# The gate operation between the two halves of a weight remainder, in the expert loop of a two-layer decoder kernel

## What is computed

```python
def swiglu(h, w1, w3, w2):
    a = jax.nn.silu(jnp.einsum('bsd,df->bsf', h, w1)) * jnp.einsum('bsd,df->bsf', h, w3)
    return jnp.einsum('bsf,fd->bsd', a, w2)

for e in range(N_EXPERTS):
    y = y + gates[..., e:e + 1] * swiglu(h, w1[e], w3[e], w2[e])
```

## Time and profile before

| | before |
|---|---|
| median of 3 runs | 1457.12 us (1455.85 to 1460.83) |
| profiled execution, own time | 1462.09 us |
| span of its profile | 1460.3 us |
| TensorE busy | 1441.4 us (99%) |
| VectorE busy | 1133.1 us (78%) |
| ScalarE busy | 944.8 us (65%) |
| DMA | 437.21 MB, mean 299 GB/s; 377 GB/s from 600 to 1400 us |
| chain that ended last | TensorE 83%, issue 8%, DMA 4%, VectorE 4%, ScalarE 1% |

### The profile page before, as it was taken

The page is one execution under the profiler, slowest core; times in us unless marked ns, Lnnn a source line. Parts: engine busy times, 40 slices in busy tenths (PEclk is TensorE's granted clock), DMA queues, the critical chain, the costliest instruction groups (busy, mean ns, idle before and its releaser), DMA issues.

```text
span 1460.3 us, 19714 instructions
## 1 busy us (share of the span) xinstructions
PE 1441.4 (99%) x7542; PEld 1200.4 (82%) x7542; DVE 1133.1 (78%) x968; ACT 944.8 (65%) x844; POOL 35.4 (2%) x22
## 2 busy tenths in 40 slices
PE   9999999999999999999999999999999999999998
PEld 7998888888886787887888888888888888888886
DVE  6985664454476788988888898888888888898895
ACT  7633643443476766766777777777777777677774
POOL 0000000000000000000000001000000000000000
PEclk9999999999999999999999999999999999999999
DMA  9510666544542499999999999999999999999993
GB/s 360 206 58 28 237 220 219 191 172 146 176 162 83 152 362 364 386 364 348 377 368 386 391 373 380 372 375 376 386 383 372 387 393 367 386 389 372 369 391 149
DMA packets 183873, 437.21 MB, mean 299 GB/s; under 512 B 4880, under 2 KB 6416, under 8 KB 183824
## 3 DMA queue, kind: packets, MB, share of 16 engines
q1 hardware_dynamic: 180496, 426.11, 79.1%
q0 software_dynamic: 2336, 8.39, 2.1%
q10 hardware_dynamic: 992, 2.05, 0.4%
HBM read 431.29 MB, written 5.24 MB: 299 GB/s over the span
## 4 chain that ended last, share of the span: by engine, by line
PE 83%; issue 8%; DMA 4%; DVE 4%; ACT 1%; POOL 0%; DVEq 0%; ACTq 0%; SPq 0%; POOLq 0%
PE ps L272 26%; PE ps L274 25%; PE ps L273 25%; DMA raw<-in_od_moe_w 3%; DVE wlo L261 1%; PE ps L452 1%; DMA out<-arena,slot_tok 1%; ACT whi L255 1%; PE ps L991 1%; PE ps L840 0%; PE ps L1188 0%; DVE hTlo L316 0%; PE ps L2102 0%; DVE small L1418 0%; PE ps L333 0%
## 5 line engine op out<-in xcount | busy, mean ns | idle before, releaser
L261 DVE TENSOR_TENSOR wlo<-raw,whi 128x2048 fp32r<-128x2048 f32 x406 | 905.8, 2272 | 170.6 <-ACT whi L255 168.3
L255 ACT CAST whi<-raw 128x2048 fp32r<-128x2048 f32 x406 | 750.5, 1898 | 210.8 <-DMA raw<-in_od_moe_w 151.3
L272 PE MATMUL ps<-whi,hThi 128*128 128x512 f32 (+1 forms) x1240 | 490.2, 395 | 0.3
L274 PE MATMUL ps<-whi,hTlo 128*128 128x512 f32 (+1 forms) x1240 | 482.7, 389 | 0.0
L273 PE MATMUL ps<-wlo,hThi 128*128 128x512 f32 (+1 forms) x1240 | 482.5, 389 | 0.0
L274 PEld LDWEIGHTS ps<-whi,hTlo 128*128 128x128 f32 x1240 | 233.6, 188 | 48.7
L272 PEld LDWEIGHTS ps<-whi,hThi 128*128 128x128 f32 x1240 | 233.8, 189 | 47.3 <-issue 1.2
L273 PEld LDWEIGHTS ps<-wlo,hThi 128*128 128x128 f32 x1240 | 233.9, 189 | 45.8 <-issue 0.2
L272 PE MATMUL ps<-whi,aThi 128*128 128x512 f32 x560 | 219.3, 392 | 0.0
L274 PE MATMUL ps<-whi,aTlo 128*128 128x512 f32 x560 | 218.2, 390 | 0.0
L273 PE MATMUL ps<-wlo,aThi 128*128 128x512 f32 x560 | 217.9, 389 | 0.0
(11 more groups left out here) (308 smaller groups left out, 759.4 us busy)
## 6 DMA issues: line engine op xcount, KB each, us to landing
raw<-in_od_moe_w SPq DMA_DIRECT2D x168, 2048.0 KB, 9.6
raw<-in_ev_ffn_w SPq DMA_DIRECT2D x21, 2048.0 KB, 7.8
raw<-in_ev_w_in SPq DMA_DIRECT2D x6, 2048.0 KB, 13.1
raw<-in_ev_w_out SPq DMA_DIRECT2D x2, 2048.0 KB, 8.5
raw<-in_od_w_in SPq DMA_DIRECT2D x2, 2048.0 KB, 7.8
raw<-in_od_w_out SPq DMA_DIRECT2D x2, 2048.0 KB, 8.1
raw<-in_ev_w_in SPq DMA_DIRECT2D x2, 1024.0 KB, 8.6
xres<-in_x SPq DMA_DIRECT2D x2, 512.0 KB, 4.3
```

The costliest lines, as they stand in the source:

```text
L255: act.copy(whi[s][:, part], raw[s][:, part]).then_inc(hi_ready, 1)
L261: dve.tensor_tensor(wlo[s][:, part], raw[s][:, part], whi[s][:, part].bitcast(F32), ALU.subtract).then_inc(lo_ready, 1)
L272: pe.matmul(to, lhi, rhi, start=first, stop=False)
L274: return pe.matmul(to, llo, rhi, start=False, stop=last)
```

## The change

In every step of every expert VectorE now runs the first half of the next w1's remainder, the gate, and then the second half. Before, only the last step of the last expert did so. The flag that told this step apart goes away for VectorE. Nothing on another engine changes, and no wait is added or taken out; only their order on VectorE is another. The operations that some steps add behind the gate now stand behind the second half.

```diff
-            def step(q, e, i, split_w3=True, after_gate=None, ending=False):
+            def step(q, e, i, split_w3=True, after_gate=None):
...
-                split_lo(dve, w2 + 1, 2, halves=(0,) if ending else (0, 1))
+                split_lo(dve, w2 + 1, 2, halves=(0,))
                 dve_gate(dve, 1, w3, gates(q, e, i))
-                if ending:
-                    split_lo(dve, w2 + 1, 2, halves=(1,))
+                split_lo(dve, w2 + 1, 2, halves=(1,))
                 if after_gate:
                     after_gate()
...
-                step(q, e, NF - 1, after_gate=None if last else lambda: gathered(n + 1), ending=last)
+                step(q, e, NF - 1, after_gate=None if last else lambda: gathered(n + 1))
```

## The result

The changed kernel takes 1479.01 us (median of 5 runs, 1475.98 to 1480.56), the kernel before 1457.56 us in the same comparison (5 runs, 1455.85 to 1465.07). The ratio is 1.013, 95% interval 1.0103 to 1.0157: **slower by 1.3%, about 20 us**. On another chip, later, the same kernel took 1473.35 us, ratio 1.0098 (1.0062 to 1.0134). The forecast of 1456.2 us and its range up to 1460.5 us are missed.

What follows compares the result with a forecast made beforehand. TensorE was taken to bound almost every step, the weight stream just keeping up. Of 6.9 us of gate stalls, 1.9 fit a median run; about half, 1 us, off 1457.12 gave 1456.2 us, range 1453.0 to 1460.5.

Steps and rivals of the forecast that it cites:

- The step that failed: Weight-buffer loop against TensorE's step: the delay makes 15.9 us into 16.5, under 16.70, so only reserve is lost.
- The sum: One buffer's loop: 9.2 us load, 1.95 ScalarE's lead, 4.49 VectorE's halves, 0.23 to the next issue; 15.9 us.
- The gate stalls, 6.9 us: TensorE's two turns waiting for VectorE's gate, with clock dips, cost 3.03 and 3.85 us; an earlier gate takes the idle.
- the 1.9 us of the sum: Room for gate stalls in a median run: 6.9 less 4.97 us; about half counted as won, 1 us.
- What is late next: At the down projection, the w2 remainder's reserve of 3.08 to 3.56 us limits what the removed stalls can gain.
- VectorE early, 1.35 us late: Where TensorE has not finished w3, VectorE waits before the gate and the second half ends 1.35 us late.
- The helpers, nothing: Select, indexed and gathered, now behind the second half, come at most 1.35 us later and cost nothing.
- The cover of 2.2 us: Time from the end of `gathered` to the turn ahead of its user on TensorE, said to cover the 1.35 us delay.
- Rival 2: Late w1 issue makes the down projection wait for the w2 remainder in three disturbed places: 1465 us, chance 0.12.
- So only 0.6 us is added: Argument against the slower case: in disturbed steps VectorE isn't ahead of TensorE, so the delay is only 0.6 us.
- the signs named for being wrong: Turn still waits 2 us; calm stretch's step no longer 16.70 us; median moves by more than 4.4 us.
- The rule weighed: Weight load time by the skill's rule, 2.0 us plus bytes over 436 GB/s: 6.8 us; the trace's 9.2 was used.

Runs made afterwards that it cites:

- e7: The changed kernel with each expert weight load as two 1 MB DMAs, each released by its own remainder half, ScalarE starting per half; 1454.26 us, ratio 0.9956.
- e12: The kernel before, with only SyncE's issue of the w3 load also waiting for the remainder of the transposed activations; 1480.72 us, ratio 1.015.
- e13: The kernel before, VectorE's order untouched, with only SyncE's issue of the w1 load waiting for the gate, 0.60 us; 1473.64 us, ratio 1.0097.
- e6: The kernel before with each expert weight load as two 1 MB DMAs, each released by its own remainder half, ScalarE starting per half; 1454.49 us, ratio 0.9968.
- e3: The changed kernel with select, indexed and gathered right behind the gate, ahead of the second half; 1481.28 us, ratio 1.0139.
- e9: The changed kernel plus an unneeded VectorE operation of 0.60 us behind the second half; 1466.26 us, ratio 1.0039.
- e11: The changed kernel as it stands, run again as the control beside the kernel before; 1473.35 us, ratio 1.0098.

## Why the prediction was wrong

**The step that failed** is "Where VectorE is late, the loop is 16.5 us, still under 16.70 ... The steps lose reserve, and no time by this alone." The mechanism in it was right: the second half 0.6 us late, through `lo_ready`, to the w1 load. The sum was mis-sized in one term, the load: 9.2 us from issue to landing, the median of a calm stretch. Its mean in before over the 50 steps is 9.84 us. With 0.1 us from landing to rounding, which the sum left out, 1.94 and 4.71 us, the loop was 16.6 us and not 15.9; with 0.60 it is 17.2, over TensorE's step. Measured are 17.25 to 17.3. And before's own mean step was 16.94, not 16.70: no reserve of 0.8 us was there, only 0.35. The 16.70 was too small as well, being TensorE's shortest step and not its mean: where it never waits (e7), the seven steps of an expert take 16.70, 17.09, 16.70, 16.72, 16.70, 17.46 and 16.73 us from turn to turn, 16.87 on average. Against that the loop of 16.6 us had some 0.3 us to spare, half of the 0.60. The price: 0.31 to 0.36 us a step over before's 16.94, times 54, 17 to 19 us.

**Behind it a missing limit.** The loop was treated as one slot's affair. Three slots share one stream. Even with a lead of 4 us or more a load lands 5.3 us behind the one ahead (the median in before and in the changed kernel), 15.9 us a step, so the other two slots have little with which to fill the hole that a late one leaves. e12 and e13 show the cost for two of the three slots, w3's and w1's.

**The gate stalls, 6.9 us.** Their mechanism was right as far as the gate comes earlier. They didn't go: the changed kernel has four, 5.2 us. In each of them the gate stands right behind its first half, which had itself waited 2.3 to 5.3 us for ScalarE, and ScalarE 2.6 to 5.6 us for the w1 load. The price of a stall as about twice its length (1.53 us made 3.03) doesn't carry over either: the clock fell behind one of the 14 stalls of the changed kernel. (The first dip of before lasted 3.4 us and not 3.00, so it cost 1.7 us and not 1.50.) The room in a median run was more than the 1.9 us of the sum, too: with no stall at all, e6 and e7 are 5.3 and 5.6 us under before's median beside them. "What is late next" named the w2 remainder; it is there (8 times, 5.2 us), and the start of the w1 product beside it.

**VectorE early, 1.35 us late.** Didn't occur: no gate wait for TensorE after, where 10 to 25 us had been forecast. It does in e7 (40.0 us), where the stream has slack, and costs nothing there.

**The helpers, nothing.** The cover of 2.2 us was that of a calm kernel; 6.8 us of waits stand there now. But e3 shows them to be mainly the same lateness, so the price of nothing was about right, for the wrong reason.

**Rival 2**, slower, had 0.12. Its start was right (late w1 issue, TensorE waits for the w2 remainder), its place wrong: it was to be three disturbed spots, 1465 us, and was every step. "So only 0.6 us is added" was counted against it; 0.6 us was enough. Of the signs named for being wrong, two came: the turn still waits 2 us (2.1 at the longest), and the median moved by more than 4.4 us. The third decides nothing: TensorE still has steps of 16.70 us between its waits, while the stream's mean step went from 16.94 to 17.3.

**The rule weighed.** By the Trainium skill, "DMA: Bandwidth & Descriptors", section on the anatomy of one DMA, the load would be an estimated 6.8 us. Mean issue to landing is 9.5 to 10.5 us in before, the changed kernel, e9, e11 and e13, further from it than the 9.2 us that I took. The page gives its fit for one DMA issued by GpSimd; these loads are issued by SyncE with another load still under way, so the figure can't stand for them, and no run here tests it on its own ground. The same page, in its rules for kernel authors, wants at least 1 MiB per DMA for bandwidth; e7's 1 MB loads stay at that bound and moved 379 GB/s with TensorE full, which agrees.

## What to carry to other kernels

A loop of load, process, release has a reserve only against its mean over the whole phase, disturbances in, not against the calm stretch's median; take every term as the mean, and compare with the bounding engine's mean step, not with its shortest. If the consumers of the loads wait for them in most steps already (100 waits here before the change), anything that is put in front of a release can cost in every step: 0.60 us here cost 0.12 to 0.40 us a step in the different runs, and in the changed kernel 14 to 21 us in all. The cure here was to free a buffer in parts, as its parts are done, which made the order irrelevant and the kernel 5 us faster.

## What the runs showed of the hardware

A 2 MB load that is issued 4 us or more before the landing of the one ahead lands 5.3 us after it (median in both kernels; means 5.47 us before, 5.38 us changed). In the changed kernel a w1 load with a lead under 3.6 us lands 6.47 us after it on average; in the example the stream drops to 172 to 266 GB/s for 2 us. I had taken a queue with one load under way for full. Two loads of 1 MB in place of one of 2 MB cost the stream nothing that these runs can tell: 379 and 380 GB/s, TensorE without a gap, and in e7 ScalarE's waits for loads of 4.3 us in all. A stall of TensorE of 1.53, 2.18 or 2.09 us was followed by 3.4 us at the granted clock of 0.50, one of 2.04 us was not; which idles bring the lower clock these runs leave open.
